# Thirty-two experts in order of their row counts: four blocks of 96 rows, then blocks of 64 rows in two strips

## The reference, cut to what matters

```python
logits = h @ w_router + b_router            # 384 x 32
top_val, top_idx = lax.top_k(logits, 4)
gate = softmax(top_val)
def expert_block(tok, e):
    gu = h[tok] @ w_gate_up[e] + b_gate_up[e]      # 1024 -> 2048
    return clamped_swiglu(gu) @ w_down[e] + b_down[e]   # 1024 -> 1024
# y[token] += gate * expert output, over the token's four experts
```

## Time and profile before

| | us |
|---|---|
| median of three runs (lowest, highest) | 1486.15 (1481.61, 1490.94) |
| the profiled execution | 1482.21 |
| its span, first to last instruction | 1480.2 |
| PE busy in it | 1377.6 |
| DVE, ACT, POOL busy | 320.1, 211.8, 145.9 |

### The profile page before, as it was taken

How to read it: one execution, slowest core, us unless ns; L and a number is a source line. 1 busy time by engine, 2 the same in 40 slices (tenths; PEclk the granted TensorE clock), 3 DMA queues, 4 the chain that set the end, 5 groups by cost and what they waited for, 6 DMA issues and landing times.

```text
span 1480.2 us, 31680 instructions
## 1 busy us (share of the span) xinstructions
PE 1377.6 (93%) x13542; PEld 682.8 (46%) x13542; DVE 320.1 (22%) x701; ACT 211.8 (14%) x519; POOL 145.9 (10%) x212
## 2 busy tenths in 40 slices
PE   3799999985899999999999999999999999999992
PEld 0685567862244444444444444444444444444441
DVE  0112345544111211111111122112111111211113
ACT  1212445030100100100000010001000000100101
POOL 2003000600000000011000000000100000000010
PEclk9899999985999999999999999999999999999996
DMA  9928742621899999999999999999999999999953
GB/s 313 367 88 301 291 153 70 238 100 64 288 366 403 391 393 392 391 394 376 391 381 399 395 392 392 395 392 393 384 383 385 385 396 394 382 397 391 371 194 106
DMA packets 122514, 483.84 MB, mean 327 GB/s; under 512 B 12486, under 2 KB 15782, under 8 KB 105222
## 3 DMA queue, kind: packets, MB, share of 16 engines
q1 hardware_dynamic: 109280, 449.71, 77.7%
q0 software_dynamic: 9488, 25.62, 7.6%
q10 hardware_dynamic: 3718, 8.12, 1.6%
HBM read 471.69 MB, written 19.32 MB: 332 GB/s over the span
## 4 chain that ended last, share of the span: by engine, by line
PE 90%; DMA 3%; DVE 3%; ACT 1%; SPq 1%; issue 1%; ACTq 0%; DVEq 0%; POOLq 0%
PE ps L1693 45%; PE ps L1725 22%; PE ps L1367 5%; PE ps L1395 4%; PE ps L1604 3%; DMA ring<-in_ada_w 3%; PE ps L1684 2%; PE ps L1506 2%; SPq L505 1%; PE ps L1563 1%; PE ps L1357 1%; PE ps L1438 1%; PE ps L1706 1%; PE ps L1625 0%; PE ps L1564 0%
## 5 line engine op out<-in xcount | busy, mean ns | idle before, releaser
L1693 PE MATMUL ps<-ring_r,xT 128*32 128x512 f32 x4608 | 502.3, 594 | 0.0
L1725 PE MATMUL ps<-ring,aT 128*32 128x384 f32 (+1 forms) x4608 | 337.5, 450 | 0.0
L1693 PEld LDWEIGHTS ps<-ring_r,xT 128*32 128x32 f32 x4608 | 138.3, 110 | 346.0 <-issue 339.3
L1725 PEld LDWEIGHTS ps<-ring,aT 128*32 128x32 f32 x4608 | 227.0, 110 | 100.2
L1693 PE MATMUL ps<-ring,xT 128*32 128x512 f32 x1536 | 170.3, 592 | 0.0
L1264 DVE TENSOR_SCALAR glu<-ps 128x768 f32<-128x768 f32 x32 | 30.6, 957 | 643.9 <-PE ps L1693 643.9
L900 ACT COPY xT<-ps 128x384 f32<-128x384 f32 x66 | 28.4, 482 | 710.2 <-PE ps L1367 710.2
L663 POOL DMA_INDIRECT y_sum<-y_blk,cur_row x32 | 46.4, 1451 | 833.6 <-DVE y_blk L1288 826.4
L1693 PEld LDWEIGHTS ps<-ring,xT 128*32 128x32 f32 x1536 | 46.0, 110 | 118.8 <-issue 118.8
L1285 DVE COPY y_blk<-ps 32x256 f32<-32x256 f32 x96 | 41.0, 427 | 230.1 <-PE ps L1725 229.2
L922 ACT ACTIVATE y_blk<-ps,cur_w 96x768 f32<-96x768 f32 x32 | 28.7, 897 | 299.2 <-PE ps L1725 299.2
(11 more groups left out here) (248 smaller groups left out, 846.6 us busy)
## 6 DMA issues: line engine op xcount, KB each, us to landing
ring<-in_moe_w SPq DMA_DIRECT2D x192, 1024.0 KB, 8.6
ring_r<-in_moe_w SPq DMA_DIRECT2D x192, 1024.0 KB, 9.2
ring<-in_ada_w SPq DMA_DIRECT2D x24, 1024.0 KB, 14.1
ring<-in_in_w SPq DMA_DIRECT2D x6, 960.0 KB, 13.3
latT<-in_cache_lat_t SPq DMA_DIRECT2D x8, 512.0 KB, 3.7
lat<-in_cache_lat SPq DMA_DIRECT2D x8, 512.0 KB, 4.5
ring<-in_out_w SPq DMA_DIRECT2D x4, 1024.0 KB, 12.3
y_sum<-qabs POOLq DMA_DIRECT2D x5, 384.0 KB, 7.6
```

Source lines behind the costliest of these rows:

```text
L1693: ins = nc.tensor.matmul(ps[strip(j), r, :], xT[:, kt, strip(group)], piece(w[:, c // 2], c % 2), start=False, stop=(kt == GU_UNITS - 1))
L1725: return nc.tensor.matmul(out, stay, w[:, cols], start=False, stop=(kt == KT - 1))
```

## The change

Blocks are taken in a new order: expert 0 first (its weights are loaded before the routing is known), the others by falling row count. The first WIDE = 4 blocks hold 96 rows and are computed as before. All others hold SMALL = 64 rows: two strips of 64 columns of the array, both with the same rows, and each with one half of the weights' columns. Their bias, activation and output instructions shrink to 64 rows or two banks. Rows above a block's capacity go to overflow blocks of 64 rows (there can now be up to 23 in place of 15, so the tables have 56 columns in place of 48). DVE computes the order from the counts; the table `order` holds the expert of each block, and SP reads from it which expert's weights to ask for. The gather still has 96 slots; a small block's `add_rows` moves 64 rows.

```diff
+WIDE = 4
+SMALL = 64
+HALVES = 2
-NOVF = NT * P * TOPK // (CAP + 1)
+NOVF = NT * P * TOPK // (SMALL + 1)
...
-        refill_gu(1, 1)
-        with sp.Fori(1, NE - 1) as i:
-            refill_gu(i + 1, i + 1)
-            refill_dn(i, i)
         sp.wait_ge(S["table_ready"], 1)
...
+        def expert_of(i):
+            return sp.value_load(order[0:1, bass.ds(i, 1)], min_val=0, max_val=NE - 1)
+
+        refill_gu(1, expert_of(1))
+        with sp.Fori(1, n_ovf + NE - 1) as i:
+            refill_gu(i + 1, expert_of(i + 1))
+            refill_dn(i, expert_of(i))
+        refill_dn(n_ovf + (NE - 1), expert_of(n_ovf + (NE - 1)))
...
-        with pool.Fori(1, n_ovf + NE) as i:
+        with pool.Fori(1, WIDE + 1) as i:
             gather(i + 1)
-            add_rows(i - 1)
-        add_rows(n_ovf + (NE - 1))
+            add_rows(i - 1, CAP)
+        with pool.Fori(WIDE + 1, n_ovf + NE) as i:
+            gather(i + 1)
+            add_rows(i - 1, SMALL)
+        add_rows(n_ovf + (NE - 1), SMALL)
...
+        key, rank_of, cap, left = rtr[:, 0, :], rtr[:, 1, :], rtr[:, 2, :], rtr[:, 3, :]
+        nc.vector.memset(key[:, 0:1], 1e6)
+        step(nc.vector.scalar_tensor_tensor(key[:, 1:NE], cnt[:, 1:NE], float(NE), expert_id[:, 1:NE], ALU.mult, ALU.subtract))
+        v.wait_ge(S["h_stored"], 16 * NT)
+        pairs = hq_again[:, 0:NE * NE].rearrange("p (e f) -> p e f", e=NE)
+        step(nc.vector.tensor_tensor(pairs, key.unsqueeze(1).to_broadcast([P, NE, NE]),
+                                     key.unsqueeze(2).to_broadcast([P, NE, NE]), ALU.is_gt))
+        step(nc.vector.tensor_reduce(rank_of, pairs, AX, ALU.add))
+        step(nc.vector.tensor_scalar(cap, rank_of, float(WIDE), float(CAP - SMALL), ALU.is_lt, ALU.mult))
+        step(nc.vector.tensor_scalar(cap, cap, float(SMALL), None, ALU.add))
+        step(nc.vector.tensor_tensor(left, cnt, cap, ALU.subtract))
...
+        step(nc.vector.tensor_scalar(cum, left, 0.0, None, ALU.is_gt))
+        for m in range(1, NT * P // SMALL - 1):
+            step(nc.vector.scalar_tensor_tensor(alt, left, float(m * SMALL), cum, ALU.is_gt, ALU.add))
+            cum, alt = alt, cum
...
+        step(nc.vector.tensor_scalar(more[0], big3, 1.0 * SMALL, None, ALU.is_ge))
+        for m in range(2, NT * P // SMALL - 1):
+            step(nc.vector.scalar_tensor_tensor(more[1], big3, float(m * SMALL), more[0], ALU.is_ge, ALU.add))
+            more = more[::-1]
...
         last.then_inc(S["placed"], 1)
+
+        holds = hq_again[:, 0:NE * NE].rearrange("p (i e) -> p i e", i=NE)
+        step(nc.vector.tensor_tensor(holds, slot_id[:, 0:NE].unsqueeze(2).to_broadcast([P, NE, NE]),
+                                     rank_of.unsqueeze(1).to_broadcast([P, NE, NE]), ALU.is_equal))
+        step(nc.vector.tensor_tensor(holds, holds, expert_id[:, :].unsqueeze(1).to_broadcast([P, NE, NE]), ALU.mult))
+        step(nc.vector.tensor_reduce(block_expert[:, 0:NE], holds, AX, ALU.add))
+        nc.vector.tensor_copy(order[0:1, 0:NBLK], block_expert[0:1, :]).then_inc(S["table_ready"], 1)
...
+                mine = y_blk[0:SMALL, 512:D]
+                ins = nc.vector.tensor_copy(mine, ps[SMALL:P, 3, :])
...
-        def gate_up(i):
+        def gate_up(i, wide):
...
+                else:
+                    for r in range(2):
+                        for j in range(HALVES):
+                            ins = nc.tensor.matmul(ps[half_array(j), r, :], xT[:, kt, 0:SMALL], piece(w[:, j], r),
+                                                   start=False, stop=(kt == GU_UNITS - 1))
...
+        def down_small(i):
...
+                for j in range(HALVES):
+                    ins = nc.tensor.matmul(y_bank[0][half_array(j), :], aT[:, kt % 4, half_array(kt // 4)],
+                                           w[:, j * 512:(j + 1) * 512], start=False, stop=(kt == KT - 1))
...
-        with pe.Fori(1, n_ovf + NE) as i:
-            expert_block(i)
-        down(n_ovf + (NE - 1))
+        with pe.Fori(1, WIDE) as i:
+            expert_block(i, True, True)
+        expert_block(WIDE, False, True)
+        with pe.Fori(WIDE + 1, n_ovf + NE) as i:
+            expert_block(i, False, False)
+        down_small(n_ovf + (NE - 1))
```

More of the change, by code:

```diff
@@ L902, in take_x, with take_act, swish, put_y @@
             ins.then_inc(S["xT_ready"], 1)
[L904 removed]
+        def take_act(i, wide):
             a.wait_ge(S["aT_filled"], i + 1)
[L907 to L909 removed]
+            if wide:
+                for r in range(2):
+                    ins = nc.scalar.copy(aT[:, 3 * r:3 * r + 3, :],
+                                         turn_bank[r][:, 0:3 * P].rearrange("p (k n) -> p k n", k=3))
+            else:
+                ins = nc.scalar.copy(aT[:, 0:4, :], turn_bank[0].rearrange("p (k n) -> p k n", k=4))
             ins.then_inc(S["aT_ready"], 1)
[L912 removed]
+        def swish(i, wide):
             a.wait_ge(S["glu_ready"], i + 1)
[L915 to L917 removed]
+            n = NG if wide else HALVES
+            nc.scalar.activation(sig[:, 0:n, :], glu[:, 0:n, :], ACT.Sigmoid, scale=1.702).then_inc(S["sig_done"], 1)
+        def put_y(i, wide):
             a.wait_ge(S["cur_w_ready"], i + 1)
@@ L1194, in _ @@
         nc.vector.memset(block_expert[:, NBLK - 1:NBLK], 0.0)
[L1195 to L1198, removed]
+        nc.vector.tensor_reduce(block_expert[:, NE:NE + NOVF], ovf, AX, ALU.add)
@@ L1200, in _ @@
+        nc.vector.tensor_copy(order[0:1, NBLK:NBLK + 1], cum[0:1, NE - 1:NE])
         first = alt
         step(nc.vector.tensor_tensor(first, cum, n_own, ALU.subtract))
[L1202 to L1206, removed]
@@ new lines, in of_expert @@
+        def of_expert(row):
+            return row.unsqueeze(1).to_broadcast([P, NT, NE])
+        step(nc.vector.tensor_tensor(big1, rank, of_expert(cap), ALU.is_ge))
+        step(nc.vector.tensor_tensor(big2, big1, of_expert(cap), ALU.mult))
+        step(nc.vector.tensor_tensor(pos, rank, big2, ALU.subtract))
+        nc.vector.tensor_tensor(blk, big1, of_expert(first), ALU.mult)
+        step(nc.vector.tensor_tensor(big3, rank, of_expert(cap), ALU.subtract))
+        step(nc.vector.tensor_tensor(blk, blk, of_expert(rank_of), ALU.add))
@@ L1666, in turn_act @@
             blocks = act[:, :, :].rearrange("p b n -> p (b n)")
-            for m in range(6):
-                ins = turn(turn_bank[m // 3][:, (m % 3) * P:(m % 3 + 1) * P], blocks[:, m * P:(m + 1) * P])
+            per_bank = 3 if wide else 4
+            for m in range(6 if wide else 4):
+                ins = turn(turn_bank[m // per_bank][:, (m % per_bank) * P:(m % per_bank + 1) * P], blocks[:, m * P:(m + 1) * P])
             ins.then_inc(S["aT_filled"], 1)
@@ L1677, in piece @@
             return cols[:, :, c * CH:(c + 1) * CH]
-        def gate_up(i):
+        def gate_up(i, wide):
             pe.wait_ge(S["sel_gu_ready"], i + 1)
-            for r in range(NG):
-                for j in range(4):
-                    ins = nc.tensor.matmul(ps[strip(j), r, :], sel_gu[:, :], piece(gu_bias, r if j < NG else NG), start=True, stop=False)
+            if wide:
+                for r in range(NG):
+                    for j in range(4):
+                        ins = nc.tensor.matmul(ps[strip(j), r, :], sel_gu[:, 0:G], piece(gu_bias, r if j < NG else NG),
+                                               start=True, stop=False)
+            else:
+                for r in range(2):
+                    for j in range(HALVES):
+                        ins = nc.tensor.matmul(ps[half_array(j), r, :], sel_gu[:, :], piece(gu_bias, 2 * j + r),
+                                               start=True, stop=False)
             ins.then_inc(S["gu_bias_done"], 1)
```

174 lines of the change are left out of this document (96 added, 78 removed).

## The result

Before 1486.69 us (median of 4 runs, 1481.61 to 1490.94), after **1447.62 us** (4 runs, 1442.67 to 1452.38): the ratio is 0.9743, 95% interval 0.9709 to 0.9776. The profiled execution after took 1443.3 us, its span is 1441.5; against the span of 1480.2 that is 38.7 us less, where the prediction's sum had 49.

The account below looks back on a forecast made before the run. PE was taken to pace the blocks at 33.8 us, transfers next at 33.5. Blocks -32.4, lead -25, last accumulate -0.5 and routing +8.5 made -49 us from 1482.2: 1433, stated as 1434, range 1408 to 1472.

Parts of the forecast that it names:

- the likeliest case: Whole kernel: the forecast itself holds, 1408 to 1452 us, chance 0.70.
- the rate of the blocks: Small blocks at the transfers' pace: 32.6 us each in place of 33.8, over 27 blocks 32 us less.
- the wide blocks: Blocks 0 to 3, still 96 rows: taken to stay as they are, no time gained or lost.
- the lead: End of the kernel: time from block 30's transfers done to PE's last `down`, 36.8 us before, 11.7 after, 25 less.
- the routing: Before the expert blocks, with PE idle: computing the order adds 8.5 us (6 to 11).
- the rest: End of the kernel: last accumulate of 64 rows in place of 96 and its copies, 0.5 us less.
- TensorE: PE work of a small block: two strips of 64 columns run side by side, 22.8 us in place of 33.8.
- a deep queue moves less: Weight loads, rival: with eleven outstanding their average falls to 372 GB/s, a block takes 35.1 us, total 1500; chance 0.05.
- The bounds: Time of a small block: at most 33.8 us, at least 30.8 where nothing is lost beside the accumulate.
- The rival at 1765: PE in small blocks: clock stays at 1.2 GHz, some 44 us of PE work a block, 280 us more; chance 0.03.
- The memory limit: Transfers of small blocks: at about 358 GB/s a block takes 36.4 us, total 1536; given no chance of its own.
- Transfers gain nothing: Small blocks, rival: they stay at 33.8 us and only the lead goes, 17 us less, 1465 to 1469; chance 0.18.

Follow-up runs that it names:

- kernel with the third bank: Changed kernel with a third bank of `gate_up` products that nobody reads, 6.9 us more PE work per small block: 1451.24 us, ratio 0.9743.
- kernel with 96 rows added: Changed kernel, but the accumulating transfer of a small block moves all 96 rows again in place of 64: 1464.78 us, ratio 0.984.

## Why the prediction was right, and where its sizes were not

1434 was forecast and 1448 came, inside the range and inside the likeliest case's own (to 1452). The mechanism was right in the signs that were named: the first product of `gate_up` 6.3 us later (8 was named), PE busy 240 us less, landing times above 20 us, share at 1.02, PE waiting for loads, 12.4 us from block 30's transfers to the last `down`. Of the 11 us that are missing from the 49, the rate of the blocks makes 6.8, the wide blocks 4.0 and the lead 2.6; the routing, half a microsecond of the rest and rounding give 2.6 back.

*TensorE.* Two strips of 64 columns do run side by side: the group of 192 products is gone, and a unit of eight takes 1.96 us in the chain where 13.73 / 8 = 1.7 was expected. The kernel with the third bank shows that even 6.9 us of error would have been free.

*The lead.* 25.1 expected, 22.5 measured. The prediction took block 30's transfers to be done by 1414.5, from a share of 0.02 over the next 15.5 us; the trace has the last landing at 1416.3, so the lead was 34.9 us and not 36.8. The kernel with 28 wide blocks shows the term nearly by itself: 22 us less by the medians, although the routing adds 7. It is the safest term, since it was read from two rows (the last landing, the last product) and needed no rate.

*The rate*, the step that takes 13.17 MB at 423 GB/s as 31.1 us, adds the 2.4 us lost beside POOL's transfers, and takes 0.3 and 0.55 off. It gave 32.6 us a block, and 33.0 came: 25.6 us for 27 blocks where 32.4 were expected. The kernel with 96 rows added splits the gain. It has the transfers of before and no PE that paces, and a block of 33.7, where the prediction had these transfers at 33.5: the reserve behind PE's 33.8 was 0.1 us and not 0.3. The 32 rows then gave 0.7, where the prediction had 0.85.

A finer look shows that two larger errors stand behind this small one. I divided the stretch from 700 to 1300 of both traces in slices of 1 us and took those without a packet of POOL's queue apart. Before, 438 such slices at 418 GB/s, and 162 others at 314; after, 488 at 409 and 112 at 345. Per block that is, before, 13.17 MB / 418 = 31.5 and 9.1 us x (1 - 314 / 418) = 2.3 lost, 33.8 in all; after, 13.04 / 409 = 31.9 and 6.2 us x (1 - 345 / 409) = 1.0 lost, 32.9. The loss beside POOL's transfers fell by 1.3 us and not by 0.55. But the bytes needed 31.9 us and not 30.8: 423 had been one stretch of one block, a good one (0.4 us), and the clean rate after is 2% lower (0.7 us). That the two errors nearly cancel is luck. (For the kernel before, this only shares out PE's 33.8: its loads could move no more than PE asked for.)

Is the lower clean rate the rival "a deep queue moves less"? If it were, that would be 0.7 us a block, where the rival needed 1.8 (34.4 against 32.6) to decide. But it is not shown. The kernel with 28 wide blocks, where a load lands in 11.6 us, has a clean rate of 414; the one with 64 gathered positions, where it takes 22.7, has 414 too, and the other kernels with two short pieces and small blocks from the fifth on have 405 to 410. The longer pieces bring it to 419, with the same full queue. What the 2% hang on stays open.

*The bounds* held: 30.8 to 33.8 for a block. The accumulate was rightly named as the source of the blocks' gain: with its 32 rows back, block and ratio are nearly those of no gain. Why it gains is another matter. The prediction priced rows and bytes. Three pairs of kernels differ by 18 skipped rows a block, the second also by the moved operations. At the prediction's price of 0.3 us for the bytes of 32 rows that is 0.2 us a block, 5 us in all; the pairs show 1.6, 0 and 3 us (0.9732 against 0.9743, 0.9637 against 0.9637, 0.9563 against 0.9583), none clear of nothing. So the part of the bytes is small and not shown, and the term may have come out because 32 positions went with the 32 rows.

*Routing.* 8.5 expected, 7.0 measured: from the writing of `chosen` to the first product of `gate_up` it is 26.2 us before and 33.2 after. (The first refill is only 6.3 later, since this trace reached the routing 0.7 us earlier.) The 1024-element operations took 1.22 us each, not 1.4. Two rows of the timeline's groups, from 334 to 368:
```profile
L1197 DVE TENSOR_TENSOR hq_again<-rtr 128x1024 f32<-128x1024 f32 x1 | 1.2, 1225 | 0.0
L1199 DVE TENSOR_REDUCE rtr<-hq_again 128x32 f32<-128x1024 f32 x1 | 1.2, 1220 | 0.0
```
It was scaled in proportion from 480 elements, and the two sizes together (0.66 and 1.22 us) leave a part of some 0.15 us that does not grow. Five such operations make 0.9 us of the missing 1.5.

*The wide blocks* were taken to stay as they are. In this trace the last `down` load of block 3 landed 4.0 us later against the first refill than before, in seven others with the same wide blocks and pieces 1.1 to 2.4 later. The prediction had nothing here; 1 to 2 us may be real, and their cause is open.

*The clock.* The rival at 1765 is refuted. Over 600 us the granted clock was 0.99 with PE busy for 77% of it, and in the fall at 559.8 PE, once its load had landed, worked without a break, and the level rose. The Trainium skill's page "TensorE: Matmul & The Clock Gate", section "HAM oscillation — how this bites in real kernels", warns of a fall with each tile's wait where that wait is longer than the tile's work. The trace agrees that a stretch with little work (1.33 of 3.4 us) is followed by half clock, and shows that waits of 0.6 us between units of 1.94 us don't bring it, as from 1386 to 1391 (timeline: start, duration, what, idle before it), at full clock:
```profile
1388.60 1.94 PE L1753 MATMUL ps<-ring,xT 128*64 128x512 f32 x8 [0.63 <-DMA ring<-in_moe_w]
...
1391.12 1.94 PE L1753 MATMUL ps<-ring,xT 128*64 128x512 f32 x8 [0.58 <-DMA ring<-in_moe_w]
```
And the kernel with the third bank, whose clock was 1.00 from 700 to 1300, had the same time. One reading of the prediction rests on durations alone: it calls the first 34 us of the kernel before slow throughout, where the earlier trace rows has a granted clock of 1.00. The trace's clock records begin at 38.4 us, so that 1.00 says nothing there.

*The memory limit.* The Trainium skill's page "DMA: Bandwidth & Descriptors", section "Specifications", gives a core about 358 GB/s. The trace disagrees: 397 GB/s over 600 us, 405 with the longer pieces.

*Transfers gain nothing* was refuted at its number: that case is the kernel with 96 rows added, 0.984, against 0.9743 with the intervals apart.

## What to carry to other kernels

When one engine is made a third faster and the next bound is 1% behind, look for the time between the last landing and the last use: that lead is given back once, down to what the last loads themselves need (34.9 to 12.4 us here), and can be read from two rows, while what follows at the new bound must be worked out from its mean rate over many blocks and not from its best stretch. Once loads pace a kernel, the shape of the transfers is worth more than their last bytes: another layout with longer contiguous pieces (16 us here by the ratios) and fewer positions in an indirect transfer (14 us by itself, about 6 beside the other), while positions that merely move nothing gave none that could be told. And a theory that two kernels agree with should still be sent a third that its rival would win.

## What was not expected of the hardware

- One piece of 8 KB per partition instead of two of 4 KB, in another place in memory, took a load of 1 MB from 2.56 to 2.49 us between landings, and the mean rate from 397 to 405 GB/s.
- An accumulate that moves 18 rows of 4 KB fewer, its count of positions unchanged, gave the loads beside it nothing that could be told (0.9732 against 0.9743); 16 positions fewer gave 1% (0.9651), as did 32 empty positions fewer in the gather (0.9649).
- In the changed kernel a row of the accumulate holds a DMA engine for 0.33 us, nearly twice as long as a gathered row of the same 4 KB (0.16 to 0.2).
- SP's own issue of a 4 KB-piece load took up to 5.6 us while the queue was full (4.51 in the piece of line 468 shown); no run separates what this costs from the full queue itself, though the chain of waits passes through SP's issues for 46% of the span.
